# A fused two-block transformer kernel: tile 2 turned under the next unit, weight splits and copies reordered, last rows by column halves

## The chip, the cores and the metric

One core of a Trainium2 chip runs the whole program in one launch. The metric is the device time in microseconds (us); the median of three runs before the change is 1148.49 us (1148.07 to 1149.39).

## What is computed

256 tokens of width 1024, in fp32, go through two blocks. Cut to what matters:

```
h = x + 0.5*rms(swiglu(rms(x)))                       # FFN 1, D_FF 2816
z, xbc, dt, q, k, v, gates = split(rms(h) @ w_in)     # first mixer
y_ssd = rms_by_group(ssd(silu(conv(xbc)), dt) * silu(z)) @ w_branch
y_att = rms(differential_attention(q, k, v)) @ w_branch
h = h + rms((sig(g0)*y_ssd + sig(g1)*y_att) @ w_out)
h = h + 0.5*rms(swiglu(rms(h)))                       # FFN 2
qa, ka, va, q_lat, kv_lat, k_r, ga, gb = split(rms(h) @ w_in_2)
x = h + (sig(ga)*(swa(qa,ka,va) @ w_o1) + sig(gb)*(mla(...) @ w_o2)) @ w_out_2
x = x + swiglu(rms(x))                                # FFN 3
out = rms(x)
```

rms is a root-mean-square norm with a gain row.

## The kernel before

**Units and the ring.** All weights stream in units of 128 x 2048 words (1 MB) through a ring of five slots. SP issues the load of unit c when `w_used` says that unit c - 5 is done. ACT rounds it (`split_hi`, L435 to L443: WH, the high part), DVE subtracts (`split_lo`, L949 to L957: WL, the low part), and PE uses both: `parts` (L1567 to L1569) makes one fp32-like product from three matmuls, high x high, high x low, low x high. Splits are handed out in the order of the units, and where each stands among the other work of ACT and DVE is written out by hand. A split in the wrong place makes PE wait for it, or makes what stands behind it late.

**Tiles.** The tokens are two tiles of 128. H is the residual, XN the normed rows, XTH and XTL the normed rows turned (K on the partitions) and split. Eight PSUM banks: PS[0] to PS[3] are ACC (down projections, two banks for each tile), PS[4] and PS[5] take gate and up products, PS[6] and PS[7] the turned rows.

**FFN.** `ffn` runs 11 steps of 256 hidden columns: units a and b (gate and up, upper and lower half of K) and d (down). The last three d units run by tiles, t = 0 for all three, then t = 1. In step j PE waits for the first tile of step j - 1's hidden rows (`h_ready`), which DVE makes (L999) from ACT's silu (L498).

**Boundary and norm.** Behind each FFN or output product, `boundary(m)` on ACT and DVE makes the post-norm, the residual and the next normed rows, tile 1 then tile 2: ACT squares (L513), rstd (L516, L517), DVE gain and residual (L1015, L1022), ACT squares and rstd of H (`h_rstd`, L464 to L466), DVE XN (L969, L971), PE turns (`turn_normed`, L1501), ACT copies XTH (`xn_hi`, L472), DVE XTL (L978). Meanwhile `norm(n, c)` on PE runs the first two units on tile 1: the high parts of unit c (L1514, L1515), then the low (L1518), then half of unit c + 1 with the first turn of tile 2 in its middle, and then tile 2. n = 1 goes before the first mixer's projection, n = 2 before FFN 2, n = 3 before the second projection, n = 4 before FFN 3. The unit that follows is a narrow one of 32 columns (`narrow`, the step sizes dt) at n = 1, and a chunk of 512 columns at n = 3.

**First mixer.** Projection units XZ (z, dt, x with convolution on DVE, L1166), then q, k, v units beside the scan: for r = 0 to 8, PE, ACT, DVE and POOL each do one step of a group and chunk of the scan, then `beside(r)` units of q, k, v and gate 0. After that 8 heads of attention, each beside one unit of `ssd_w_branch`, and then the gates: for n = 0 to 3, DVE adds the bias (L1327), ACT takes the sigmoid (L740), and both split two units for n = 1 to 3.

**Second mixer.** Rotary terms, latents, 16 heads in two kinds, with g2, kv and output pieces as `cover(q)` between heads.

**End.** Boundary 4 adds FFN 3's rows to H, squares, and DVE scales each tile with gain and rstd (L1484); SP stores each tile (L426).

Of the kernel before, what the change touches and what calls it, by code (L numbers as in the profile page):

```python
# [184 lines left out]
def program(nc, w, out):  # L185
    with ExitStack() as ctx:
# [101 lines left out]
        out_ok = sem("out_ok")  # L288
# [46 lines left out]
        def in2_bank(n, t):  # L335
            return ((4, 5), (0, 1), (4, 5))[n][t]

# [10 lines left out]
        def _(sp):  # L348
# [75 lines left out]
            for t in range(NT):  # L424
                sp.wait_ge(out_ok, t + 1)
                sp.dma_start(x_out[:, t, :], XN[:, t, :]).then_inc(stored, 16)  # L426
            sp.wait_ge(stored, 16 * NT)

        @block.scalar
        def _(act):  # L430
# [89 lines left out]
            def boundary(m, unit, half, next_table=None):  # L520
# [3 lines left out]
                if m in (1, 3):  # L524
# [48 lines left out]
            def x_hi(t):  # L573

                act.wait_ge(ident_loaded, 32)
                for q in range(2):
                    act.wait_ge(xn_turned, 2 * t + q + 1)
                    for k in range(4 * q, 4 * q + 4):
                        ins = nc.scalar.activation(XTH[:, k, t * P:(t + 1) * P], PS[6 + q][:, k % 4 * P:(k % 4 + 1) * P],
                                                   ACT.Copy, scale=COLS[:, k:k + 1])  # L580
                    ins.then_inc(xt_hi, 1)
# [10 lines left out]
            x_hi(0)  # L592
# [16 lines left out]
            for m, (kind, n, h) in enumerate(XZ):  # L609
# [45 lines left out]
            def qkv(u):  # L655
# [8 lines left out]
                elif n < 8:  # L664
                    act.wait_ge(w_used, u + 1)
                    nc.scalar.activation(QK[:, 2 * (n % 4):2 * (n % 4) + 2, n // 4, :],
                                         PS[5 - n % 2][:].rearrange("p (f t) -> p f t", f=2),
# [9 lines left out]
            for r in range(9):  # L677
# [154 lines left out]
            for q in range(18):  # L832
# [5 lines left out]
                if q < 16:  # L838
                    head_exp(q)
                if q in (0, 1, 2, 4, 6, 8, 10, 11, 12, 14, 15, 16, 17):  # L840
# [14 lines left out]
                elif q == 16:  # L855
                    act.wait_ge(tile_half, HALF[U_OSWA])
                    kt_hi(18, U_OSWA)
# [12 lines left out]
            boundary(4, U_END - 1, False)  # L870
# [73 lines left out]
        def _(dve):  # L944
# [89 lines left out]
            def boundary(m, unit, gains=0):  # L1034
# [45 lines left out]
            def x_lo(t):  # L1080

                dve.wait_ge(ident_loaded, 32)
                for q in range(2):
                    dve.wait_ge(xt_hi, 2 * t + q + 1)
                    for k in range(4 * q, 4 * q + 4):
                        a = XTH[:, k, t * P:(t + 1) * P]
                        ins = stt(XTL[:, k, t * P:(t + 1) * P], PS[6 + q][:, k % 4 * P:(k % 4 + 1) * P], COLS[:, k:k + 1],
                                  a.bitcast(F32), ALU.mult, ALU.subtract)
                    ins.then_inc(xt_lo, 1)
# [10 lines left out]
            x_lo(0)  # L1100
            first_unit_lo()
            x_lo(1)
            split_lo()
            split_lo()
# [12 lines left out]
            def step_sizes(c):  # L1117
# [4 lines left out]
                   PS[2][:].rearrange("p (t c) -> p t c", t=NT)[:, :, 0:32], bias, ALU.add).then_inc(dt_raw, 1)  # L1122
# [68 lines left out]
            for r in range(9):  # L1191
# [37 lines left out]
                for _u in range(beside(r)):  # L1229
                    split_lo()  # L1230
            kt_lo(0)
# [919 lines left out]
```

## Time and profile before

| | |
|---|---|
| median of three runs | 1148.49 us |
| the profiled execution | 1148.1 us |
| its span, first to last instruction | 1146.3 us |
| mean granted TensorE clock | 0.992 |
| PE busy | 1116.1 us, 97%, 5748 matmuls |
| PE weight loads | 940.8 us, 82% (beside PE) |
| DVE busy | 697.5 us, 61% |
| ACT busy | 593.6 us, 52% |
| POOL busy | 20.8 us, 2% |
| bytes moved | 202.23 MB, mean 176 GB/s |

Busy time is time in which the engine executes; a share of 97% means that only 3% of the span is open to anything but fewer or faster matmuls. Durations of single matmuls overlap, so their spacing, not their duration, is their cost. L1567 is line 1567 of the kernel before.

### The profile page before, as it was taken

How to read it: one execution, taken by the hardware profiler on the slowest of the kernel's cores; microseconds unless marked ns; L12 is line 12 of the kernel's file. 1: busy time of each engine (PE TensorE's matmuls, PEld its weight loads, DVE VectorE, ACT ScalarE, POOL GpSimd, SP SyncE). 2: the span in 40 equal slices, each digit the busy share in tenths (PEclk: the TensorE clock that was granted, in tenths of full speed). 3: DMA queues.
4: the chain of work that ended last, by engine and by line, in shares of the span. 5: the costliest groups of instructions: out<-in, count | busy, mean ns of one | idle time of the engine just before them, and what ended most of it. 6: DMA issues, size and time to landing. Idle time of an engine off the chain costs nothing.

```text
span 1146.3 us, 14028 instructions
## 1 busy us (share of the span) xinstructions
PE 1116.1 (97%) x5748; PEld 940.8 (82%) x5748; DVE 697.5 (61%) x807; ACT 593.6 (52%) x843; POOL 20.8 (2%) x34
## 2 busy tenths in 40 slices
PE   6999999999999999998999999999999999999997
PEld 4888888899999987777878888887878878888886
DVE  4645555676767777866756455555775667554453
ACT  5543435454567766646445434445766546344442
POOL 0000000000001100000000000000000000000000
PEclk9999999999999999999999999999999999999999
DMA  7755654655566545444466555544634445555550
GB/s 259 251 187 185 189 191 138 225 172 181 182 200 182 171 164 202 133 162 164 149 198 205 185 189 191 190 155 146 205 125 129 153 160 173 192 186 184 184 184 37
DMA packets 132208, 202.23 MB, mean 176 GB/s; under 512 B 5889, under 2 KB 98945, under 8 KB 131889
## 3 DMA queue, kind: packets, MB, share of 16 engines
q1 hardware_dynamic: 129472, 190.68, 51.7%
q0 software_dynamic: 2672, 10.65, 2.8%
q8 instruction: 46, 0.75, 0.3%
q14 instruction: 18, 0.14, 0.0%
HBM read 200.24 MB, written 1.08 MB: 176 GB/s over the span
## 4 chain that ended last, share of the span: by engine, by line
PE 90%; DVE 4%; ACT 4%; issue 1%; DMA 1%; SPq 0%; DVEq 0%; ACTq 0%
PE PS L1567 14%; PE PS L1569 14%; PE PS L1568 14%; PE ACC L1567 13%; PE ACC L1569 13%; PE ACC L1568 13%; ACT WH L442 1%; PE PS L1628 1%; DVE WL L957 1%; PE PS L1501 1%; PE ACC L1815 1%; PE PS L1972 1%; PE PS L1667 1%; PE PS L1971 0%; DMA RAW<-in_w_out 0%
## 5 line engine op out<-in xcount | busy, mean ns | idle before, releaser
L957 DVE TENSOR_TENSOR WL<-RAW,WH 128x2048 fp32r<-128x2048 f32 (+2 forms) x180 | 404.0, 2265 | 112.4 <-ACT WH L442 112.2
L442 ACT ACTIVATE WH<-RAW 128x2048 fp32r<-128x2048 f32 (+2 forms) x180 | 336.0, 1888 | 23.6 <-DMA RAW<-in_w_up 6.2
L1567 PE MATMUL PS<-WH,XTH 128*128 128x512 f32 (+1 forms) x680 | 272.3, 400 | 9.9 <-DVE WL L957 5.4
L1569 PE MATMUL PS<-WH,XTL 128*128 128x512 f32 (+1 forms) x680 | 267.0, 393 | 0.0
L1568 PE MATMUL PS<-WL,XTH 128*128 128x512 f32 (+1 forms) x680 | 266.6, 392 | 0.0
L1567 PE MATMUL ACC<-WH,KTH 128*128 128x512 f32 (+1 forms) x452 | 178.9, 396 | 0.5 <-ACT BUF L778 0.3
L1569 PE MATMUL ACC<-WH,KTL 128*128 128x512 f32 (+1 forms) x452 | 175.7, 389 | 0.0
L1568 PE MATMUL ACC<-WL,KTH 128*128 128x512 f32 (+1 forms) x452 | 175.4, 388 | 0.0
L1567 PEld LDWEIGHTS PS<-WH,XTH 128*128 128x128 f32 x680 | 129.3, 190 | 36.8 <-DVE WL L957 6.1
L1569 PEld LDWEIGHTS PS<-WH,XTL 128*128 128x128 f32 x680 | 129.1, 190 | 27.4
L1568 PEld LDWEIGHTS PS<-WL,XTH 128*128 128x128 f32 x680 | 129.4, 190 | 24.8
L1567 PEld LDWEIGHTS ACC<-WH,KTH 128*128 128x128 f32 x452 | 84.9, 188 | 18.9 <-DVE KTL L1059 1.3
L487 ACT ACTIVATE KTH<-PS 128x512 fp32r<-128x512 f32 x30 | 17.9, 597 | 157.8 <-PE PS L1628 157.8
L1569 PEld LDWEIGHTS ACC<-WH,KTL 128*128 128x128 f32 x452 | 84.8, 188 | 17.7
L1568 PEld LDWEIGHTS ACC<-WL,KTH 128*128 128x128 f32 x452 | 85.0, 188 | 16.1
L990 DVE TENSOR_TENSOR KTL<-PS,KTH 128x512 fp32r<-128x512 f32 x30 | 20.7, 691 | 117.5 <-ACT KTH L487 117.5
L498 ACT ACTIVATE SCR<-PS,RS 128x256 f32<-128x256 f32 x66 | 31.3, 475 | 110.6 <-PE PS L1569 110.5
L999 DVE SCALAR_TENSOR_TENSOR SCR<-PS,RS,SCR 128x256 f32<-128x256 f32 x66 | 31.4, 480 | 41.2 <-ACT SCR L498 41.2
L1567 PE MATMUL ACC<-WH,XTH 128*128 128x512 f32 (+1 forms) x144 | 56.0, 389 | 0.0
L1567 PE MATMUL ACC<-XTH,WH 128*128 128x256 f32 x192 | 55.5, 289 | 0.0
L1568 PE MATMUL ACC<-XTL,WH 128*128 128x256 f32 x192 | 55.0, 286 | 0.0
L1569 PE MATMUL ACC<-XTH,WL 128*128 128x256 f32 x192 | 55.0, 286 | 0.0
(275 smaller groups left out, 1305.1 us busy)
## 6 DMA issues: line engine op xcount, KB each, us to landing
RAW<-in_w_in SPq DMA_DIRECT2D x50, 1024.0 KB, 5.2
RAW<-in_ffn_w_gate SPq DMA_DIRECT2D x44, 512.0 KB, 4.0
RAW<-in_ffn_w_up SPq DMA_DIRECT2D x44, 512.0 KB, 5.0
RAW<-in_ffn_w_down SPq DMA_DIRECT2D x22, 1024.0 KB, 5.0
RAW<-in_w_gate SPq DMA_DIRECT2D x22, 512.0 KB, 4.0
RAW<-in_w_up SPq DMA_DIRECT2D x22, 512.0 KB, 5.0
RAW<-in_w_down SPq DMA_DIRECT2D x11, 1024.0 KB, 4.8
RAW<-in_ssd_w_branch SPq DMA_DIRECT2D x8, 1024.0 KB, 5.0
```

What stands on the lines that cost most here:

```text
L442: nc.scalar.activation(WH[:, s, 0:n], RAW[:, s, 0:n], ACT.Copy).then_inc(w_hi, 1)
L487: nc.scalar.activation(KTH[:, half_of(j)], PS[6][:], ACT.Copy).then_inc(hT_hi, 1)
L498: nc.scalar.activation(SG[:, t, :], PS[4 + t][:, 0:256], ACT.Silu, scale=RS[:, t:t + 1]).then_inc(gate_ok, 1)
L957: tt(WL[:, s, 0:n], RAW[:, s, 0:n], WH[:, s, 0:n].bitcast(F32), ALU.subtract).then_inc(w_lo, 1)
L990: tt(KTL[:, half_of(j)], PS[6][:], KTH[:, half_of(j)].bitcast(F32), ALU.subtract).then_inc(hT_lo, 1)
L999: stt(HS[:, t, :], PS[4 + t][:, 256:512], RS[:, t:t + 1], SG[:, t, :], ALU.mult, ALU.mult).then_inc(h_ready, 1)
L1501: ins = nc.tensor.transpose(PS[6 + q][:, k * P:(k + 1) * P], src[:, t, j * P:(j + 1) * P], IDENT)
L1567: mm(ps, stat_hi, mov_hi, start=first, stop=False)
L1568: mm(ps, stat_hi, mov_lo, start=False, stop=False)
L1569: return mm(ps, stat_lo, mov_hi, start=False, stop=last)
L1628: ins = nc.tensor.transpose(PS[6][:, k * TOK + t * P:k * TOK + (t + 1) * P], HS[:, t, k * P:(k + 1) * P], IDENT)
L1667: ins = nc.tensor.transpose(PS[7][:, k * P:(k + 1) * P], src[:, t, (k0 + k) * P:(k0 + k + 1) * P], IDENT)
```

## The change

Nine edits; no product is added or removed.

1. Start: XTH and XTL of tile 2's two halves have the split of unit 1 between them on ACT and DVE.
2. Boundaries 0 and 2: the split that stood last on ACT and DVE now stands before the squares of tile 2 (ACT) and before XN of tile 2 (DVE). In `norm` at n = 1 and n = 3 PE finishes unit c + 1 on tile 1 first and has tile 1's part of the next unit, in two pieces, around the first turn. dt moves to bank 1, the chunk's first tile stays in bank 0.
3. Boundary 1 on ACT: XTH of tile 2 before the squares of tile 2's H and the table load. In `norm` at n = 2 the first turn stands behind three quarters of the half instead of two.
4. The last z copies stand before a split; the first q unit writes bank 0 and waits for a convolution, not for those copies.
5. Scan's last step: the first K rows (`turn_rows(0)`, `kt_hi(0)`, `kt_lo(0)`) are turned and split between the two halves of gate unit 0, not behind them.
6. Gates: ACT splits two units before the first sigmoid and then 1, 1, 2; DVE one between the two pairs of output scalings, then 1, 1, 1, 2.
7. Second mixer: the keys are turned before the first g2 piece.
8. Heads' end: `kt_hi(18)` and `kt_lo(18)` before that step's split; the first MLA output unit runs tile 2 first, so the wait for the last gate (`g2_kept` 8) comes 12 products later.
9. End: the last unit's tile 2 runs by column halves, so DVE adds, ACT squares and DVE applies the gain for half the columns while PE does the other; rstd comes from both; DVE and ACT scale one half each; two DMAs of 512 columns store it.

```diff
 # ACT, boundary
                     if m == 1:
                         y_rstd(m, unit, 1, half)
-                    h_rstd(m + 1, 0)
-                    h_rstd(m + 1, 1)
-                    nc.scalar.preload_act_table(next_table)
-                    xn_hi(m + 1, 1)
+                        h_rstd(m + 1, 0)
+                        xn_hi(m + 1, 1)
+                        h_rstd(m + 1, 1)
+                        nc.scalar.preload_act_table(next_table)
+                    else:
...
                 y_rstd(m, unit, 1, half)
+                split_hi()
                 h_rstd(m + 1, 1)
                 xn_hi(m + 1, 1)
-                split_hi()
 # ACT, start
-            x_hi(1)
+            x_hi(1, 0)
             split_hi()
+            x_hi(1, 1)
             h_rstd(0, 1)
 # ACT, z units
-                    split_hi()
+                    if (n, h) != (3, 1):
+                        split_hi()
                     if n and h:
                         z_silu(n, c - 3, c)
+                    if (n, h) == (3, 1):
+                        split_hi()
 # ACT, scan and gates
                 for _u in range(beside(r)):
+                    if u == U_GATE0 + 1:
+                        kt_hi(0, 0)
                     qkv(u)
                     u += 1
-            kt_hi(0, 0)
...
-                if n:
-                    split_hi()
+                split_hi()
+                if n in (0, 3):
                     split_hi()
 # ACT, end
-            boundary(4, U_END - 1, False)
+            ln_exp()
+            h_rstd(5, 0)
+            act.wait_ge(last_half, 1)
+            own.wait()
+            own.link(nc.scalar.activation(JUNK[:, 0:512], H[:, 1, 0:512], ACT.Square, accum_out=SS[:, 1:2]))
+            own.inc(nc.scalar.activation(SS[:, 2:3], SS[:, 1:2], ACT.Identity, scale=1.0 / D, bias=EPS))
+            act.wait_ge(last_half, 2)
+            own.inc(nc.scalar.activation(JUNK[:, 512:1024], H[:, 1, 512:1024], ACT.Square, accum_out=SS[:, 3:4]))
+            own.wait()
+            own.link(nc.scalar.activation(RS[:, 1:2], SS[:, 3:4], ACT.Ln, scale=1.0 / D, bias=SS[:, 2:3]))
+            nc.scalar.activation(RS[:, 1:2], RS[:, 1:2], ACT.Exp, scale=-0.5).then_inc(rstd_ok, 1)
+            act.wait_ge(rstd_ok, NT * 6)
+            act.wait_ge(out_gained, 1)
+            nc.scalar.activation(XN[:, 1, 0:512], XN[:, 1, 0:512], ACT.Copy, scale=RS[:, 1:2]).then_inc(out_act, 1)
 # DVE, boundary
+                if m in (0, 2):
+                    split_lo()
                 xn(m + 1, 1)
                 xn_lo(m + 1, 1)
-                split_lo()
+                if m in (1, 3):
+                    split_lo()
 # DVE, output scalings and gates
                        ALU.mult).then_inc(o_ok, 1)
+                if p == 0:
+                    split_lo()
...
-                if n:
+                if n == 3:
                     split_lo()
-                    split_lo()
+                split_lo()
 # DVE, end
+            for h in range(2):
+                dve.wait_ge(w_used, U_END) if h else dve.wait_ge(end_half, 1)
+                a = slice(h * 512, (h + 1) * 512)
+                tt(H[:, 1, a], PS[2 + h][:], H[:, 1, a], ALU.add).then_inc(last_half, 1)
+                dve.wait_ge(last_half, h + 1)
+                tt(XN[:, 1, a], H[:, 1, a], GAIN[:, a], ALU.mult).then_inc(out_gained, 1)
+            dve.wait_ge(rstd_ok, NT * 6)
+            dve.wait_ge(out_gained, 2)
+            ts(XN[:, 1, 512:1024], XN[:, 1, 512:1024], RS[:, 1:2], None, ALU.mult).then_inc(out_ok, 1)
 # PE, norm
-                half(c + 1, 1, 0, 4, (0, 1))
-                turn_normed(n, 1, 0)
-                half(c + 1, 1, 0, 4, (2, 3)).then_inc(chunk_half, 1)
+                if beside:
+                    half(c + 1, 1, 0, 4).then_inc(chunk_half, 1)
+                    pe.wait_ge(w_lo, c + 3)
+                    beside(0)
+                    turn_normed(n, 1, 0)
+                    beside(1)
+                else:
+                    ks = 3 if n == 2 else 2
+                    half(c + 1, 1, 0, 4, range(ks))
+                    turn_normed(n, 1, 0)
+                    half(c + 1, 1, 0, 4, range(ks, 4)).then_inc(chunk_half, 1)
...
-            norm(1, U_XZ)
+            norm(1, U_XZ, lambda h: narrow(U_XZ + 2, 1, SSD_HEADS, 0, range(4 * h, 4 * h + 4)))
...
-            norm(3, U_IN2)
+            norm(3, U_IN2, lambda h: half(U_IN2 + 2, 0, 0, 0, range(2 * h, 2 * h + 2)))
 # PE, heads' end
-                    pe.wait_ge(g2_kept, 8)
                     pe.wait_ge(w_lo, U_OMLA + 1)
-                    rows_part(U_OMLA, [(0, 0)], True, False, half=0)
+                    rows_part(U_OMLA, [(0, 1)], True, False, half=0)
...
-            mla_piece(0, 1)
+            pe.wait_ge(g2_kept, 8)
+            rows_part(U_OMLA, [(0, 0), (1, 0)], True, False, half=0).then_inc(w_used, 1)
```

## Rows read from the trace of the kernel before

**Rows 1.** Waits of PE: engine, line, waited for, us in total, times, longest us.

```profile
PE PS L1567 <- DVE WL L957: 5.4, 3, 3.0
...
PE PS L1501 <- DVE XN L969: 4.4, 2, 2.2
...
PE PS L1567 <- ACT BUF L607: 1.3, 1, 1.3
PE PS L1567 <- DVE XTL L978: 1.1, 1, 1.1
PE PS L1712 <- DVE KTL L1059: 0.5, 1, 0.5
```

**Rows 2.** Busy time by stretches; PEclk is the column behind POOL.

```profile
21.50:25.00 3.50, 3.41 (x8) 2.63 (x9) 1.07 (x2) 2.42 (x2) 0.00 (x0) 0.54 0.78 269
...
223.00:226.60 3.60, 3.60 (x20) 3.60 (x20) 3.21 (x6) 2.28 (x5) 0.00 (x0) 0.53 0.58 165
...
519.00:524.00 5.00, 3.69 (x10) 2.92 (x11) 3.46 (x2) 5.00 (x4) 0.00 (x0) 0.66 0.49 197
...
782.00:787.00 5.00, 4.41 (x17) 3.64 (x18) 1.89 (x3) 0.90 (x2) 0.00 (x0) 0.66 0.00 0
```

**Rows 3.** Timeline of the start: start, us, engine, line, op, [idle before <- releaser].

```profile
16.27 1.14 ACT L579 ACTIVATE XTH<-PS,COLS 128x128 fp32r<-128x128 f32 x4 [1.23 <-PE PS L1501]
...
19.25 2.29 DVE L957 TENSOR_TENSOR WL<-RAW,WH 128x2048 fp32r<-128x2048 f32 x1 [0.68 <-ACT WH L442]
...
21.59 0.63 PE L1567 MATMUL PS<-WH,XTH 128*128 128x512 f32 x1 [2.21 <-DVE WL L957]
```

**Rows 4.** Timeline of norm 1; the last two are the first and last of 48.

```profile
210.01 0.66 PE L1501 MATMUL PS<-TAB,XN 128*128 128x128 f32 x4 [2.21 <-DVE XN L969]
...
217.82 0.18 PE L1567 MATMUL ACC<-WH,XTH 128*128 128x32 f32 x1
...
222.98 0.26 PE L1569 MATMUL ACC<-WH,XTL 128*128 128x32 f32 x1
```

**Rows 5.** Timeline of the gates.

```profile
516.03 3.69 ACT L442 ACTIVATE WH<-RAW 128x2048 fp32r<-128x2048 f32 x2
...
520.31 0.79 PE L1567 MATMUL PS<-WH,XTH 128*128 128x512 f32 x1 [3.02 <-DVE WL L957]
```

**Rows 6.** Timeline of norm 2.

```profile
593.08 1.28 ACT L532 ACT_TABLE_LOAD   x1
...
594.38 1.08 ACT L472 ACTIVATE XTH<-PS 128x512 fp32r<-128x512 f32 x2
...
595.35 1.92 ACT L442 ACTIVATE WH<-RAW 128x2048 fp32r<-128x2048 f32 x1
595.75 0.50 PE L1567 MATMUL PS<-WH,XTH 128*128 128x512 f32 x1 [1.07 <-DVE XTL L978]
...
599.51 0.48 DVE L999 SCALAR_TENSOR_TENSOR SCR<-PS,RS,SCR 128x256 f32<-128x256 f32 x1
```

**Rows 7.** Timeline of boundary 2: H of tile 2.

```profile
778.81 1.28 DVE L1022 SCALAR_TENSOR_TENSOR H<-SCR,RS,H 128x1024 f32<-128x1024 f32 x1
```

**Rows 8.** Timeline of the heads' end: a split and what it waited for.

```profile
918.67 1.91 ACT L442 ACTIVATE WH<-RAW 128x2048 fp32r<-128x2048 f32 x1 [3.62 <-DMA RAW<-in_w_out]
```

**Rows 9.** Timeline of the end; the first two are 12 matmuls.

```profile
1135.98 0.39 PE L1567 MATMUL ACC<-WH,XTH 128*128 128x512 f32 x1
...
1138.48 0.39 PE L1569 MATMUL ACC<-WH,XTL 128*128 128x512 f32 x1
...
1138.97 1.29 DVE L1030 TENSOR_TENSOR H<-ACC,H 128x512 f32<-128x512 f32 x2 [6.87 <-PE ACC L1569]
...
1141.95 1.28 DVE L1484 SCALAR_TENSOR_TENSOR XN<-H,RS,GAIN 128x1024 f32<-128x1024 f32 x1 [0.49 <-ACT RS L466]
...
1143.26 0.36 SPq L426 DMA_DIRECT2D out_x<-XN  x1
```

**Rows 10.** Waits of ACT, the hidden rows of all FFNs.

```profile
ACT KTH L487 <- PE PS L1628: 157.8, 27, 6.3
```

More of the change, by code:

```diff
@@ L336, in in2_bank, with q_bank @@
             return ((4, 5), (0, 1), (4, 5))[n][t]
+        def q_bank(n):
+            return 5 - n % 2 if n else 0
         def v_bank(n, t):
@@ L423, in _ @@
             ffn_loads(U_FFN3, w["w_gate_2"], w["w_up_2"], w["w_down_2"])
[L424 to L427, printed above, removed]
+            sp.wait_ge(out_ok, 1)
+            sp.dma_start(x_out[:, 0, :], XN[:, 0, :]).then_inc(stored, 16)
+            sp.wait_ge(out_ok, 2)
+            sp.dma_start(x_out[:, 1, 512:1024], XN[:, 1, 512:1024]).then_inc(stored, 16)
+            sp.wait_ge(out_act, 1)
+            sp.dma_start(x_out[:, 1, 0:512], XN[:, 1, 0:512]).then_inc(stored, 16)
+            sp.wait_ge(stored, 48)
         @block.scalar
@@ L570, in products, with x_hi @@
                         split_hi()
-            def x_hi(t):
+            def x_hi(t, q):
                 act.wait_ge(ident_loaded, 32)
[L576 to L581, printed above, removed]
+                act.wait_ge(xn_turned, 2 * t + q + 1)
+                for k in range(4 * q, 4 * q + 4):
+                    ins = nc.scalar.activation(XTH[:, k, t * P:(t + 1) * P], PS[6 + q][:, k % 4 * P:(k % 4 + 1) * P],
+                                               ACT.Copy, scale=COLS[:, k:k + 1])
+                ins.then_inc(xt_hi, 1)
             def first_unit_hi():
@@ L1078, in products, with x_lo @@
                             split_lo()
-            def x_lo(t):
+            def x_lo(t, q):
                 dve.wait_ge(ident_loaded, 32)
[L1083 to L1089, printed above, removed]
+                dve.wait_ge(xt_hi, 2 * t + q + 1)
+                for k in range(4 * q, 4 * q + 4):
+                    a = XTH[:, k, t * P:(t + 1) * P]
+                    ins = stt(XTL[:, k, t * P:(t + 1) * P], PS[6 + q][:, k % 4 * P:(k % 4 + 1) * P], COLS[:, k:k + 1],
+                              a.bitcast(F32), ALU.mult, ALU.subtract)
+                ins.then_inc(xt_lo, 1)
             def first_unit_lo():
@@ L1580, in channels, with narrow @@
                 ins.then_inc(w_used, 1)
-            def narrow(c, bank, wide):
+            def narrow(c, bank, wide, t, ks):
                 s = slot(c)
-                pe.wait_ge(w_lo, c + 1)
-                for t in range(NT):
-                    for k in range(KD):
-                        ws = slice(k * wide, (k + 1) * wide)
-                        ins = parts(PS[bank][:, t * 256:t * 256 + wide], x_hi(k, t), x_lo(k, t),
-                                    WH[:, s, ws], WL[:, s, ws], k == 0, k == KD - 1)
-                ins.then_inc(w_used, 1)
+                for k in ks:
+                    ws = slice(k * wide, (k + 1) * wide)
+                    ins = parts(PS[bank][:, t * 256:t * 256 + wide], x_hi(k, t), x_lo(k, t),
+                                WH[:, s, ws], WL[:, s, ws], k == 0, k == KD - 1)
+                return ins
             def rows_part(c, order, first, last, banks=0, half=0):
@@ L1653, in ffn @@
                         half_at = 2 if n == 2 else (s + n) % 2
-                        rows_part(c, [(0, t)], False, n == 2, half=half_at)
-                        if t and n == 2 and then:
-                            then()
-                        ins = rows_part(c, [(1, t)], False, n == 2, half=half_at)
+                        if t and n == 2 and f == 2:
+                            for h in range(2):
+                                for k in range(2):
+                                    ws = slice(k * D + h * 512, k * D + (h + 1) * 512)
+                                    ins = parts(PS[2 + h][:], LASTH[:, 2 * k + 1], LASTL[:, 2 * k + 1], WH[:, slot(c), ws],
+                                                WL[:, slot(c), ws], False, k == 1)
+                                if h == 0:
+                                    ins.then_inc(end_half, 1)
+                        else:
+                            rows_part(c, [(0, t)], False, n == 2, half=half_at)
+                            if t and n == 2 and then:
+                                then()
+                            ins = rows_part(c, [(1, t)], False, n == 2, half=half_at)
                         if t:
@@ L1755, in _ @@
                 elif kind == "dt":
-                    narrow(c, 2, SSD_HEADS)
+                    narrow(c, 1, SSD_HEADS, 1, range(KD)).then_inc(w_used, 1)
                 elif n and h:
```

68 lines of the change are left out of this document (42 added, 26 removed).

## The prediction

> **What bounds the kernel now.** Read first the busy table of the page: PE is busy 1116.1 of 1146.3 us, no other engine above 61%. A change that adds and removes no matmul can therefore win only where PE is dry, where its clock is low, or behind its last matmul. Then the waits of PE [rows 1]: the five rows hold 12.7 us. What else PE waits for is the first DMA and the first splits, before its first product, where the change does nothing, and five waits of 0.2 to 0.4. Most of the 12.7 lies in four places: at 21.59, 210.01, 520.31 and 782.59 us PE is dry for 2.21, 2.21, 3.02 and 2.21 us. Then the clock by stretches [rows 2]: 1.00 everywhere except four pieces, and there PE ran at 1.2 instead of 2.4 GHz for about 3.4 us. In the first, 8 matmuls started in 3.5 us where 15 fit at the full-clock spacing of (1138.48 - 1135.98) / 11 = 0.227 us [rows 2, 9]: one such stretch costs 7 x 0.227 = 1.6 us. Three of the four begin in or just behind a dry place; the fourth, at 223 us, comes right behind 48 matmuls of 32 columns, and the dry place at 210 us was followed by none for 13 us. So dry time and clock are removed together, but not for certain. Last, the tail: 1138.5 to 1146.3 us.
>
> **The change part by part.** All times are of the profiled execution: 1148.1 us, its span 1146.3 and 1.8 around it; the median shown is 1148.49, 0.4 above.
>
> *Start.* ACT is free at 16.27 - 1.23 = 15.04 us and now splits unit 1 (1.9 us) before the last quarter of XTH; DVE follows at 16.97 instead of 19.25 and ends at 19.3 [rows 3]. PE ran out at 21.59 - 2.21 = 19.38: the gap goes, and with it the half-clock stretch behind it. What is late next: XTH's last quarter, the squares (1.6), the table load and unit 2's split stand one behind the other on ACT, so WL of unit 2 is ready at 25.0 and the first hidden tile at 25.5, while PE is there at 19.4 + 24 x 0.227 = 24.85. Before, it was there at 21.59 + 5.46 + 1.6 = 28.7. Gain 28.7 - 25.5 = 3.2.
>
> *Turn of tile 2 before the first projection (norm 1).* The dry 2.21 us up to 210.01 are filled with 6 half-unit products and 12 of the 32-column ones (spacing (222.98 - 217.82) / 47 = 0.110) [rows 4]; 12 more stand between the two turns. The split of the narrow unit that DVE now does before XN is 128x256, 0.4 us, under its wait for RS. Counted on PE from 206.3: 12 x 0.227 + 1.3 + 0.4 + 1.3 + 0.4 + 24 x 0.227 + 2.6 = 14.2, so the projection begins at 220.6 and not at 223.1: 2.4. The low clock at 223 may stay (now 24 narrow products before it and 24 around the turns). If it goes, 1.6 more, less about 0.4, since the step-size chain on DVE is then late for the first turn of x. I take the middle: 3.0, ends 2.4 and 3.6.
>
> *Z copies and the first q unit.* The 1.35 us wait for both silu copies [rows 1] goes, since the unit writes bank 0. The split moved behind the copies delays DVE's cumulative columns by 2 us, and the scan's first mask has some 1.5 us of room: 1.2, ends 0 and 1.35.
>
> *End of scan.* K turns one unit earlier, so the KTL wait of 0.45 goes [rows 1], but the 4 turns no longer cover the second gate copy, and DVE is the later engine there. 0, ends -0.4 and 0.45.
>
> *Gates.* Unit 79 was split behind the first sigmoid at 516.03, its WL came at 520.3, PE was dry from 517.29 [rows 5]. Now ACT splits 79 and 80 right after the table load (510.75 to 514.4) and DVE the first between the two pairs of scalings, by 515.0; 80 by 519.6, 81 by 523.1, each before PE asks (523.0, 528.7). All of the 3.02 goes and the low clock of that place (0.66 over 5 us, so 1.4 of the 1.6): 4.4, lower end 2.5.
>
> *Boundary 1 (norm 2).* PE's waits of 0.41 and 1.07 shrink: XTH is copied when the turn is done, at 592.9 and not at 594.38, so PE goes on at 594.3 instead of 595.75 [rows 6]: +1.45. But the second squares (1.6 us) and the table load now stand between XTH and the split of unit 92. XTH ends at 594.65; squares and rstd to 596.2; table to 597.45; split to 599.4, where it began at 595.35. DVE's split and the first hidden tile behind it, which ended at 599.51 + 0.48 = 599.99, shift by the same 2.1 to 602.1. PE, which needs that tile, is there at 594.3 + 24 x 0.227 = 599.75 and is dry for 2.35 us; before, it was there at 601.2 and did not wait. Net -0.95. A dry place of this size was followed by the low clock at 21.5, 519 and 782, not at once at 210: I take half of 1.6, so -1.7; ends +1.4 (should the hidden tile be ready in time) and -2.6.
>
> At this place a rule speaks. The row shows that the table load holds ACT for 1.28 us and the next copy starts 1.30 after it [rows 6]. The Trainium skill (ScalarE: Activation LUTs, What ACT_TABLE_LOAD costs) says that a switch costs about 1283 ns plus a drain of about 1380. With the drain the new wait of PE would be an estimated 1.4 us longer and the sum 1.4 smaller. The trace has the duration, so the sum goes by it.
>
> *Boundary 2 (norm 3).* ACT splits unit 125 at 777.9 to 779.8, free there. DVE, done with H at 778.81 + 1.28 = 780.1 [rows 7], splits it for 2.29 us and only then makes XN, 0.55 later than before. PE, dry from 782.59 - 2.21 = 780.4, has 6 more products of its half now, is through at 781.6, waits 0.75 for WL at 782.35, then covers the turns with 12 products that it does later today. Of the 2.21 us 1.45 are won, of the low clock behind them 1.6 (a wait of 0.75 should not bring it: those of 1.07 and 1.35 did not), and 0.3 of slow first matmuls and fewer edges: 3.4, ends 1.4 and 3.6. DVE's queue behind that split is XN and XTL of tile 2, for which PE waits; the cover is 12 x 0.227 = 2.7 us, their chain 2.9 to the last, so little is left over.
>
> *Keys turned before the gate piece.* The 0.3 wait for the last copy goes: 0.3. *Attention's end.* The g2 wait (0.33) goes since tile 1's banks are free; but the next K copy is held on ACT by a split that starts only when a weight load has landed, at 918.67 [rows 8], and ends in PE's product at 921.85 either way: 0, upper end 0.33.
>
> *Last rows by halves.* Now: last matmul 1138.48, add of both halves, squares and rstd, XN, DMA at 1143.26, end 1146.3 [rows 9]. After: the second half's add 1138.97 to 1139.66, its square (half as long) to 1140.4, rstd to 1140.9, XN by two engines in halves to 1141.5, DMAs at 1141.4 and 1141.8. The bytes are the same, so the end comes 3.0 behind the first issue: 1144.4. Gain 1.9, ends 1.2 and 2.3.
>
> *Queues.* SP's loads wait for the same units in the same order, each as early as PE is; only the output's one DMA becomes two. POOL issues nothing else and is passed by nothing.
>
> **Sum.** 3.2 + 3.0 + 1.2 + 0 + 4.4 - 1.7 + 3.4 + 0.3 + 0 + 1.9 = 15.7. 1148.1 - 15.7 = 1132.4, and with the 0.4 to the median 1132.8 us.
>
> **The rivals.**
> A. *The new wait does not appear and the clock stays up*: +2.35 + 0.8 at norm 2 and +0.6 at norm 1: 1129.0. For it: every wait of PE but these is short. Against: the count at boundary 1 leaves 2.35 us of lateness, no rounding.
> B. *Stalls moved, not removed*: the split stream of ACT and DVE is late elsewhere by what PE wins, in the scan (slack of 1.5 us only), at unit 83 (ready within 0.1 of its use) and at norm 1, and three low-clock stretches stay. Price 1.2 + 0.6 + 3 x 1.6 = 6.6 off: 1139.4. For it: ACT and DVE chains end within a few tenths of PE in scan and heads. Against: DVE 61%, ACT 52% busy.
> C. *Slower*: FFN 2 starts with ACT and DVE 2.35 us late and they never catch up, so each of its steps stalls PE by that: 10 x 2.35 = 23.5 more: 1156. It decides when ACT's wait for the turned hidden rows falls to zero; today that wait is up to 6.3 us in a step, 157.8 in 27 [rows 10], which speaks against it.
> D. *The reordering does nothing*: the dry places are made by something the profile hides behind the named releaser. 1147. Against: the releasers' own rows end within 0.1 us of PE's starts [rows 3, 5].
>
> **How the numbers follow.** Forecast 0.64 (own range 1130 to 1136), A 0.10, B 0.20, C 0.03, D 0.03. The range 1129 to 1138.5 holds the forecast, A's edge and most of B. A difference under 0.2% (2.3 us) can't be told from none here. Faster: forecast, A, B, part of D: 0.94; same 0.03; slower 0.03.
>
> **What would show it.** In the changed kernel's waits: no PE wait for WL at the second unit or in the gates; none over 1 us for XN; one new wait of about 2.3 us for the first hidden tile of FFN 2, near 587 us plus what is won, and one near 0.7 at 25 us and at the third boundary. The clock table has one or two pieces near 0.5 in place of four, behind the narrow products or that new wait. The last DMA is issued 3.4 us behind the last matmul, now 4.8. Wrong if a boundary shows DVE's split ending after PE has run dry by more than 1 us at norm 3, if FFN 2 starts without a wait, or if the scan's mask is the releaser of a PE wait.

## The result, and the profile after

The changed kernel takes 1132.8 us (median of four runs, 1131.38 to 1134.39) against 1148.29 for the kernel before beside it (1148.07 to 1149.39): ratio 0.9859, 95% interval 0.984 to 0.9877. A second series gave 1132.72 against 1148.33, ratio 0.9867 (0.9848 to 0.9886). The forecast was 1132.8 us, and faster.

The profiled execution of after took 1134.39 us, the slowest of its four; its span is 1132.6 us (1146.3 before), mean granted clock 0.996 (0.992), PE busy 1112.1 us, 98%, the same 5748 matmuls. The waits of PE, to be laid beside [rows 1] (engine, line, waited for, us in total, times, longest):

```profile
PE PS L1620 <- DVE WL L1129: 4.1, 1, 4.1
PE PS L1620 <- DVE SCR L1029: 2.7, 2, 2.2
PE PS L1913 <- ACT BUF L677: 0.7, 1, 0.7
PE ACC L1620 <- DVE WL L987: 0.6, 1, 0.6
PE ACC L1620 <- DVE KTL L1092: 0.5, 1, 0.5
```

The first is the wait for the first split of all, before the first product (3.3 in before); the change does nothing there. Of the rows of before, DVE XN L969 (4.4) and ACT BUF L607 (1.3) are gone, DVE WL L957 (5.4) is down to 0.19 at 507.35 us and the 0.6 at norm 3, and DVE XTL L978 (1.1) to 0.3. New is the second row, 2.7 us: 2.2 of it is one wait at FFN 2. The places, on PE's timeline (start, us, line, operation, idle before and its releaser):

```profile
26.27 0.47 PE L1620 MATMUL PS<-WH,XTH 128*128 128x512 f32 x1 [0.51 <-DVE SCR L1029]
...
432.08 0.50 PE L1913 MATMUL PS<-QK 64*128 64x128 f32 x4 [0.69 <-ACT BUF L677]
...
507.35 0.47 PE L1620 MATMUL PS<-WH,XTH 128*128 128x512 f32 x1 [0.19 <-DVE WL L987]
...
593.16 0.47 PE L1620 MATMUL PS<-WH,XTH 128*128 128x512 f32 x1 [2.22 <-DVE SCR L1029]
...
774.33 0.50 PE L1620 MATMUL ACC<-WH,XTH 128*128 128x512 f32 x1 [0.62 <-DVE WL L987]
...
910.11 0.50 PE L1620 MATMUL ACC<-WH,KTH 128*128 128x512 f32 x1 [0.45 <-DVE KTL L1092]
```

The clock by stretches, beside [rows 2] (us; PE, PEld, DVE, ACT, POOL busy; PEclk; DMA share; GB/s):

```profile
19.00:26.00 7.00, 6.76 (x30) 5.03 (x28) 4.57 (x7) 4.88 (x8) 0.00 (x0) 1.00 0.70 228
208.00:213.00 5.00, 5.00 (x27) 4.43 (x27) 1.66 (x3) 2.91 (x4) 0.00 (x0) 0.68 0.41 157
219.00:224.00 5.00, 5.00 (x31) 5.00 (x31) 3.33 (x6) 4.03 (x6) 0.00 (x0) 0.66 1.07 357
592.00:597.00 5.00, 3.84 (x19) 3.21 (x20) 5.00 (x5) 3.42 (x3) 0.00 (x0) 1.00 0.85 277
774.00:779.00 5.00, 4.67 (x24) 3.90 (x25) 2.38 (x5) 1.32 (x3) 0.00 (x0) 1.00 0.00 0
```

Two pieces of half clock (stretches at 1.2 GHz) are left of four, both in norm 1 and not behind a dry place: they begin at 209.84 and 220.08 us, 0.3 and 0.4 us behind the last of 12 and of 24 matmuls of 32 columns on end. The gates, FFN 2, norm 3 and, from 15.3 us on, the start run at full clock, also behind the 2.22 us. What a piece costs is read from stage lengths (the stages are those of the table below). With one, two and three pieces norm 1 takes 34.90, 36.49 and 38.05 us in traces with PE's old order there; with none and one, norm 3 takes 31.96 and 33.49: 1.5 to 1.6 us a piece. In norm 1's new order one piece costs 1.2 (32.39 against 31.21) and two cost 2.8. The granted clock, 3.4 us at half speed each, would give 1.70.

One slow stretch the table of clocks doesn't show. In every trace of this study the first products start 0.43 us apart where the later ones start 0.23 apart, while the clock column says 1.00. Two of the kernel before:

```profile
14.03 0.63 PE L1568 MATMUL PS<-WL,XTH 128*128 128x512 f32 x1
14.46 0.63 PE L1569 MATMUL PS<-WH,XTL 128*128 128x512 f32 x1
```

The spacing falls at 15.0 us there, 5.0 behind the first product, and at 15.3 in after, 4.5 behind it.

A comparison by stages uses landmarks on PE that both kernels have (first product, first turn of norm 1, first turn of x, first scores, first turn of norm 2, first turn of hidden rows in FFN 2, first turn of norm 3, rotary turn, first scores of the second mixer, last matmul). Stages without a piece repeat from trace to trace within 0.1 us, so this is finer than the medians. Two are coarser: the start (188.9 to 189.1 in the old order), and the heads' stage, which takes 314.2 to 314.6 us with the change as it is and 314.4 to 314.7 with none of its edits in that stage.

| stage | before | after | won | forecast |
|---|---|---|---|---|
| first product to norm 1 | 191.26 | 188.11 | 3.15 | 3.2 |
| norm 1 to first turn of x | 34.90 (1 piece) | 33.98 (2 pieces) | 0.92 | 3.0 |
| to first scores (z, q, scan) | 199.92 | 199.17 | 0.75 | 1.2 |
| to norm 2 (end of scan, gates) | 149.94 | 144.86 | 5.08 | 4.4 |
| norm 2 to first hidden turn | 18.01 | 19.07 | -1.06 | -1.7 |
| FFN 2 | 169.80 | 169.82 | 0.0 | 0 |
| norm 3 and on | 33.49 | 30.39 | 3.10 | 3.4 |
| keys | 16.47 | 16.05 | 0.42 | 0.3 |
| heads, output, FFN 3 | 314.67 | 314.23 | 0.44 | 0 |
| last matmul to the end | 7.82 | 6.10 | 1.72 | 1.9 |

The sum is 14.5; the span fell by 13.7, since the first product of this execution started 0.8 us later (10.82 against 10.02).

### The profile page after: what moved, and what is told of

It reads as the page before. It is cut to its first block, busy times and chain, and to the rows that moved or that the text cites. A ratio compares the mean times of both kernels' runs of the same rounds, so it can differ in the third digit from the quotient of the medians.

```text
span 1132.6 us, 14039 instructions
## 1 busy us (share of the span) xinstructions
PE 1112.1 (98%) x5748; PEld 938.5 (83%) x5748; DVE 697.5 (62%) x809; ACT 594.6 (53%) x847; POOL 20.8 (2%) x34
## 4 chain that ended last, share of the span: by engine, by line
PE 94%; ACT 2%; DVE 2%; DMA 1%; issue 1%; SPq 0%; DVEq 0%; ACTq 0%
PE PS L1620 14%; PE PS L1622 14%; PE PS L1621 14%; PE ACC L1620 14%; PE ACC L1622 14%; PE ACC L1621 14%; PE PS L1679 1%; PE ACC L1882 1%; DVE WL L987 1%; PE PS L1546 1%; PE PS L2039 1%; DMA RAW<-in_ffn_w_up 1%; ACT WH L449 1%; PE PS L1727 1%; PE PS L2038 0%
## 5 line engine op out<-in xcount | busy, mean ns | idle before, releaser
L1620 PE MATMUL ACC<-XTH,WH 128*128 128x256 f32 x208 | 60.0, 288 | 0.0
L1621 PE MATMUL ACC<-XTL,WH 128*128 128x256 f32 x208 | 59.6, 286 | 0.0
L1622 PE MATMUL ACC<-XTH,WL 128*128 128x256 f32 x208 | 59.5, 286 | 0.0
```

The costliest lines, as they stand in the source:

```text
L1620: mm(ps, stat_hi, mov_hi, start=first, stop=False)
L1621: mm(ps, stat_hi, mov_lo, start=False, stop=False)
L1622: return mm(ps, stat_lo, mov_hi, start=False, stop=last)
```

## The experiments

**Boundary 1, from the changed kernel.** The split of FFN 2's next unit, moved early (the old place stays at m = 3 alone):

```diff
                     if m == 1:
                         y_rstd(m, unit, 0, half)
+                        split_hi()
                     xn_hi(m + 1, 0)
...
-                    split_hi()
+                        split_hi()
                     return
```

> The changed kernel with one move on ACT at boundary 1: the split of the unit of FFN 2's second step stands behind the first post-norm rstd (ACT idle there for 4.30 us up to 577.58) instead of behind the last squares and the table load. Theory (the new 2.22 us wait of PE for the first hidden tile is made by that split standing at 588.38 to 590.3 on ACT, with DVE's half of it behind): ACT's silu comes at 588.4, the hidden tile at 589.4, PE asks at 590.95 and does not wait; 1132.8 - 2.2 = 1130.6 us, interval about 0.2% wide. Rival (DVE's chain or the product's own arrival makes the tile late, the split only stands beside it): the wait stays at 1.5 to 2.2 us, 1132 to 1133. Rival 2 (the wait only moves to the next step, whose splits are as late): 1132.8 and a new wait of some 2 us near 597.

Measured: 1129.49 us (1128.72 to 1130.48), ratio to before 0.9827 (0.9809 to 0.9845). The rows of after (first fence) and of this kernel (second), ACT and DVE:

```profile
587.09 1.28 ACT L540 ACT_TABLE_LOAD   x1
588.38 1.92 ACT L449 ACTIVATE WH<-RAW 128x2048 fp32r<-128x2048 f32 x1
590.20 0.45 ACT L505 ACTIVATE SCR<-PS,RS 128x256 f32<-128x256 f32 x1
...
592.54 0.87 DVE L1029 SCALAR_TENSOR_TENSOR SCR<-PS,RS,SCR 128x256 f32<-128x256 f32 x2
```

```profile
583.58 1.28 ACT L541 ACT_TABLE_LOAD   x1
584.88 0.47 ACT L505 ACTIVATE SCR<-PS,RS 128x256 f32<-128x256 f32 x1
...
585.38 0.48 DVE L1030 SCALAR_TENSOR_TENSOR SCR<-PS,RS,SCR 128x256 f32<-128x256 f32 x1 [0.40 <-ACT SCR L505]
```

The silu stands right behind the table load now, and DVE starts on the hidden tile 1.8 us behind that load's start, where it was 5.5 behind. PE has no wait there; the stage from norm 2 to the first hidden turn is 16.53 us, 2.54 less than in after and 1.48 less than before the change. So the cause of the wait is shown, it did not move to the next step, and the price of the edit at norm 2 was only the place of one split. The medians are 3.3 apart; the rest fits the clock, 0.997 to 1.0 in the four runs of this kernel and 0.996 to 0.999 in those of after.

The edit of boundary 1 on ACT taken back, with the three quarters of the half before the first turn kept:

```diff
-                        h_rstd(m + 1, 0)
-                        xn_hi(m + 1, 1)
-                        h_rstd(m + 1, 1)
-                        nc.scalar.preload_act_table(next_table)
-                    else:
-                        h_rstd(m + 1, 0)
...
+                    h_rstd(m + 1, 0)
+                    h_rstd(m + 1, 1)
+                    nc.scalar.preload_act_table(next_table)
+                    xn_hi(m + 1, 1)
```

> The changed kernel with boundary 1 on ACT in the order of before (both squares and the table load ahead of XTH of tile 2), the first turn still behind three quarters of the half. Theory (that edit alone brings both the 1.45 us gained before the turn and the 2.22 us wait behind it, net -1 to -1.7): 1131.8 us, ends 1131.1 and 1132.1; waits for XTL of 1.0 to 1.4 back, none for the first hidden tile. Rival (the wait comes from the three quarters or from elsewhere, the ACT order is a gain): 1134.3, wait for the hidden tile stays.

Measured: 1131.33 us (1130.39 to 1133.3), ratio 0.9844 (0.9826 to 0.9863); the stage is 18.05 us, against 18.01 before and 19.07 in after. The wait for XTL is back, 1.77 us where 1.0 to 1.4 were expected, and there is none for the hidden tile:

```profile
586.56 0.50 PE L1615 MATMUL PS<-WH,XTH 128*128 128x512 f32 x1 [1.77 <-DVE XTL L1003]
```

So this edit, as it stood, cost 1.0 us, and with the split moved it gives 1.5: the sign hung on what stood behind it on ACT. The three quarters are worth nothing by themselves (18.05 and 18.01): the time saved before the turn comes back in the wait behind it.

**The 32-column matmuls spread out**, for the two pieces in norm 1:

```diff
-                if beside:
+                if n == 1:
+                    half(c + 1, 1, 0, 4, range(2))
+                    pe.wait_ge(w_lo, c + 3)
+                    beside(0, range(0, 3))
+                    half(c + 1, 1, 0, 4, (2,))
+                    beside(0, range(3, 5))
+                    turn_normed(n, 1, 0)
+                    beside(0, (5,))
+                    half(c + 1, 1, 0, 4, (3,)).then_inc(chunk_half, 1)
+                    beside(0, (6, 7))
+                elif beside:
                     half(c + 1, 1, 0, 4).then_inc(chunk_half, 1)
...
+                    for h in range(2):
+                        pe.wait_ge(xt_lo, 4 * n + 3 + h)
+                        for k in range(4):
+                            ins = half(c + h, h, 1, 5, (k,))
+                            if k == 3:
+                                ins.then_inc(w_used, 1)
+                            ins = beside(1, (4 * h + k,))
```

> The changed kernel with the 48 matmuls of 32 columns before the first projection spread between the wide ones of tile 1's and tile 2's half units, in runs of 3 to 9 instead of 12, 12 and 24. Same products. Theory (the two half-clock pieces of the changed kernel, 208 to 213 and 218 to 223 us, follow from the dense runs of narrow matmuls): both go, 2 x 1.6 us where a run has both; the repeats of the changed kernel spread over 1131.4 to 1134.4, so the median falls by 1.6 to 3.2, to 1131.2 to 1129.6, and the spread shrinks. Rival (the clock falls there by the turns and dry tenths around them, or by chance): both pieces stay, 1132.8 within 0.7.

Measured: 1134.33 us (1133.41 to 1134.48), ratio 0.9867 (0.9849 to 0.9884). The times of both expectations fail. The clock over the stretch is 1.00, but so it is in four traces of kernels that keep the dense runs (below), so this says nothing on the cause; and the order costs time. Against the kernel with the early split, whose norm 1 has full clock too (31.19 us), its stage takes 32.68. ACT and PE of this kernel, then ACT of the other:

```profile
219.03 1.91 ACT L449 ACTIVATE WH<-RAW 128x2048 fp32r<-128x2048 f32 x1 [4.74 <-DMA RAW<-in_w_in]
...
230.26 0.63 ACT L643 ACTIVATE SCR<-SCR 128x512 f32<-128x512 f32 x1 [3.36 <-DVE SCR L1200]
...
230.94 0.66 PE L1823 MATMUL PS<-TAB,SCR 128*128 128x128 f32 x4 [1.15 <-ACT SCR L643]
```

```profile
217.46 1.91 ACT L449 ACTIVATE WH<-RAW 128x2048 fp32r<-128x2048 f32 x1 [3.62 <-DMA RAW<-in_w_in]
```

The spread matmuls stand between unit c's last products, so that unit is done and the load into its slot lands 1.6 us later, and ACT's split, which waits for that load, holds the step sizes, the convolution and the turn of x behind it: 219.03 against 217.46, 230.94 against 229.38. Its trace also has a piece behind the 2.21 us wait at FFN 2, where that of after has none.

**One part of the change alone, in the kernel before.** Gates:

```diff
-                if n:
-                    split_hi()
+                split_hi()
+                if n in (0, 3):
                     split_hi()
# DVE
+                if p == 0:
+                    split_lo()
...
-                if n:
+                if n == 3:
                     split_lo()
-                    split_lo()
+                split_lo()
```

> The kernel before with the gates' edit alone (ACT splits two units ahead of the first sigmoid, DVE one between the pairs of scalings). Theory: the dry 3.02 us at 517 to 520 and the half clock behind it go together: 4.4 us faster than before, lower end 3.0 (dry time alone), upper 4.9 (what the two traces show over this stretch). Rival (the half clock stays, it comes from the thin work of the preceding stretch): 3.0. Rival 2 (ACT and DVE owe the time in the following boundary): under 2.

Measured: 1142.04 us (1141.3 to 1145.22) against 1149.03, ratio 0.994 (0.9921 to 0.9958), so 4.8 to 9.1 us faster. The stage from scores to norm 2 is 145.08 us instead of 149.94: 4.86 is what the edit gives. The rest of the profiled difference lies elsewhere: this trace has the same dry 2.21 us before norm 3 as [rows 2] and no half clock behind it.

```profile
778.19 0.66 PE L1503 MATMUL PS<-TAB,XN 128*128 128x128 f32 x4 [2.21 <-DVE XN L969]
```

```profile
778.00:783.00 5.00, 4.81 (x25) 4.07 (x26) 2.19 (x4) 2.89 (x3) 0.00 (x0) 1.00 0.00 0
```

The start (`x_hi(1, 0)`, `split_hi()`, `x_hi(1, 1)`, and the same on DVE), norm 1 and norm 3 (each with its split moved and PE's order as in the change), and the end, each alone:

> The kernel before with the start's edit alone (the last quarter of XTH and XTL behind the split of unit 1). Theory: the dry 2.21 us at 21.6 and the half clock behind it go, the first hidden tile is late by 0.5 instead: 3.2 us faster than before, ends 2.8 and 3.6. Rival (the half clock is chance and stays somewhere): 1.6 to 1.9. Rival 2 (ACT pays it back in the first steps of FFN 1): under 1.

> The kernel before with norm 1's edit alone (narrow unit's tile 1 around the first turn of tile 2, its split ahead of XN). Theory (dry 2.21 us filled with work that is done anyway): from the first turn before norm 1 to the first turn of x the time falls from 34.9 us to 31.2 where no half clock falls in it, to 34.0 where two pieces do (as in the two traces of the changed order seen so far), so 0.9 to 3.7 faster, most likely 2.5. Rival (two pieces always come with the new order): 0.9. Rival 2 (the step sizes' chain on DVE becomes late for the first turn of x): a wait of 1 us there.

> The kernel before with norm 3's edit alone (first tile of the next chunk around the first turn of tile 2, its split ahead of XN on DVE). Theory: 1.6 of the dry 2.21 us go, one wait of 0.6 for WL stays, and the half clock behind it goes if it was there: 3.1 faster than a run that has the piece at 782 us, 1.5 than one that has not (the kernel with the gates' edit alone had the same dry 2.21 us and no half clock behind them): between 1.5 and 3.1. Rival (the dry time is only moved to the turns: XN is 0.5 late behind the split): 0.5 or less.

> The kernel before with the end's edit alone (last rows by column halves). Theory: from the start of the last matmul to the end of the span 6.1 us instead of 7.8, so 1.7 faster, ends 1.4 and 2.0. Rival (the end is set by the output's last DMA, whose bytes are the same and which are now two): 0.5 or less, with the issue earlier and the end not.

Measured against 1148.82 us (29 runs, 1147.54 to 1153.18):

| alone | median, us | ratio (95%) | its stage | same stage, before |
|---|---|---|---|---|
| start | 1146.18 | 0.9973 (0.9961 to 0.9984) | 187.83 | 191.26 with a piece, 188.9 to 189.1 without |
| norm 1 | 1143.97 | 0.9952 (0.9935 to 0.9968) | 32.39, 1 piece | 34.90 with 1 piece, 36.49 with 2 |
| norm 3 | 1146.21 | 0.9977 (0.9964 to 0.9989) | 30.43 | 33.49 with a piece, 31.9 without |
| end | 1147.49 | 0.9978 (0.9966 to 0.9991) | 6.09 | 7.82 |

All four are faster; the medians alone could not rank them, since runs of the kernel before differ by more than five microseconds, with mean clocks of 0.992 or 0.993 up to 1149.1 us and of 0.989 from 1151.4 us on. The stages can. Norm 1 gives 2.5 us at an equal number of pieces (34.90 - 32.39, and 36.49 - 33.98); its median shows more than any theory allowed, and its trace has no half clock at the start, where nothing was edited: PE was dry there for 1.65 us, not 2.21, as in the traces of norm 3 and the end alone. In these three the matmuls came to full speed 3.3 to 3.8 us behind the first product and not 5.0, so the turns of tile 2, and ACT's copies and split behind them, were early: PE could go on 11.02 us behind the first product (norm 1 alone) and not 11.57. Of the 2.15 us between 191.26 and 189.11, 0.55 is this and 1.6 the piece. Norm 3 is 3.06 where a piece goes with it and 1.5 where not; one wait for WL of 0.61 stays, and XN is not late:

```profile
783.06 0.50 PE L1581 MATMUL ACC<-WH,XTH 128*128 128x512 f32 x1 [0.61 <-DVE WL L960]
```

The end comes earlier with the issue, though the last tile's bytes are the same: last matmul, then first and second DMA of that tile. The span ends 2.7 us behind the second; before the change it ended 3.0 behind the single one.

```profile
1138.26 0.39 PE L1594 MATMUL ACC<-WH,XTL 128*128 128x512 f32 x1
...
1141.25 0.36 SPq L428 DMA_DIRECT2D out_x<-XN  x1
1141.65 0.43 SPq L430 DMA_DIRECT2D out_x<-XN  x1
```

Edits 4, 5, 7 and 8 were not run alone; what is said of them below is read from waits and stages.

**The changed kernel once more.**

> The changed kernel unchanged, once more, on the chip of the next three. Theory (what differs from run to run in it is only how many half-clock pieces of 1.7 us fall into a run, since the same dry place had one in some traces and none in others): 1131 to 1135 us, in steps of about 1.7, mean granted clock 0.996 to 0.999, the slower runs those of the lower clock. Rival (runs differ by their dry places): same clock in all runs, other waits.

Measured: 1131.0, 1131.67, 1133.76 and 1134.99 us, with mean clocks 0.999, 0.999, 0.996, 0.996. Its profiled execution (span 1129.2, 3.4 less than the first one's) has every wait of the fences above within 0.1 us, but for the start's and no piece at all:

```profile
208.00:213.00 5.00, 5.00 (x30) 4.36 (x30) 2.50 (x3) 3.85 (x4) 0.00 (x0) 1.00 0.22 84
219.00:224.00 5.00, 5.00 (x44) 5.00 (x44) 4.49 (x10) 3.70 (x9) 0.00 (x0) 1.00 0.78 257
589.00:594.00 5.00, 4.45 (x22) 3.70 (x23) 5.00 (x5) 3.46 (x4) 0.00 (x0) 1.00 0.73 231
```

Norm 1 takes 31.21 us here and 33.98 there: the same instructions, waits and order, and 2.8 us apart by two pieces.

**Dry places made by repeats.** The first hidden tile computed several times over, in a step where the stream is steady:

```diff
+                        for _ in range(DOSE.get((f, j), 0) if t == 0 else 0):
+                            own.link(stt(HS[:, t, :], PS[4 + t][:, 256:512], RS[:, t:t + 1], SG[:, t, :], ALU.mult, ALU.mult))
```

> The kernel with the early split at boundary 1, and in steps 3 and 7 of each FFN the first hidden tile computed 14, 16; 15, 17; 16, 18 times more on DVE (the same values again), each about 0.5 us, against a slack of 6.1 us before PE asks for the tile: dry places of about 0.9, 1.9; 1.4, 2.4; 1.9, 2.9 us in a steady stream of wide matmuls. Theory (the half clock follows long dry places and not short ones: in the traces so far it came behind 5 of 5 of 3.02 us, 9 of 14 of about 2.2, 0 of 4 of 1.6 to 1.8 and none shorter): a piece of 1.7 us behind the place of 2.9, perhaps behind that of 2.4, none behind 0.9 and 1.4. Rival (the pieces belong to the boundaries, where turns and narrow or split-starved work stand together, and not to dry time): none behind any of the six. Rival 2 (every dry place can bring it, by chance): pieces behind short ones too.

> As the kernel before it, with the repeats in other places: 17, 15; 18, 14; 15, 17, so dry places of about 2.4, 1.4; 2.9, 0.9; 1.4, 2.4 us. Theory: a half-clock piece behind 2.9, perhaps behind the two of 2.4, none behind 0.9 and 1.4. Rival: none at all, or the pieces stand at the same steps as in the other kernel whatever their dry time.

Measured: 1148.22 and 1146.86 us, one run of each kernel. Each repeat is 0.52 us, and each dry place came out 0.2 to 0.3 us longer than planned. Of the first kernel PE's rows at four places and the clock behind them, of the second two:

```profile
147.02 0.47 PE L1625 MATMUL PS<-WH,XTH 128*128 128x512 f32 x1 [2.17 <-DVE SCR L1034]
645.12 0.47 PE L1625 MATMUL PS<-WH,XTH 128*128 128x512 f32 x1 [1.65 <-DVE SCR L1034]
715.27 0.47 PE L1625 MATMUL PS<-WH,XTH 128*128 128x512 f32 x1 [2.69 <-DVE SCR L1034]
1082.55 0.50 PE L1625 MATMUL PS<-WH,XTH 128*128 128x512 f32 x1 [3.24 <-DVE SCR L1034]
```

```profile
147.00:152.00 5.00, 4.98 (x17) 4.00 (x18) 2.47 (x2) 0.00 (x0) 0.00 (x0) 0.66 0.54 187
645.00:650.00 5.00, 4.88 (x23) 4.07 (x24) 3.25 (x3) 1.41 (x2) 0.00 (x0) 1.00 0.63 207
715.00:720.00 5.00, 4.73 (x23) 3.97 (x24) 3.37 (x4) 1.28 (x2) 0.00 (x0) 1.00 0.47 162
1082.00:1087.00 5.00, 4.45 (x13) 3.48 (x14) 3.00 (x3) 0.00 (x0) 0.00 (x0) 0.66 0.41 145
```

```profile
649.27 0.47 PE L1625 MATMUL PS<-WH,XTH 128*128 128x512 f32 x1 [3.21 <-DVE SCR L1034]
```

```profile
649.00:654.00 5.00, 4.73 (x23) 3.98 (x24) 3.36 (x4) 1.28 (x2) 0.00 (x0) 1.00 0.36 125
```

Half clock came behind 2.17, 2.20 and 3.24 us and not behind 1.13 (twice), 1.65, 1.68 (twice), 2.69, 2.72 (twice) and 3.21. So the first rival (boundaries only) is wrong, the third (short ones too) has nothing for it, and the theory holds in its lower half only: a longer dry place does not make it certain. Apart from the clock, a dry place costs about 0.3 us above the idle time shown: FFN 2, where neither kernel has a piece, takes 174.69 and 174.70 us against 169.83 in the kernel without repeats, 4.9 more for 4.34 of idle time in two places.

**A version that beats both.** The early split, and at the heads' end the K copy ahead of a split that waits for a load:

```diff
+                if q == 17:
+                    kt_hi(19, U_OSWA + 2)
                 if q in (0, 1, 2, 4, 6, 8, 10, 11, 12, 14, 15, 16, 17):
                     split_hi()
...
-                elif q == 17:
-                    kt_hi(19, U_OSWA + 2)
```

> The kernel with the early split at boundary 1, and besides the copy of the K rows of the heads' end (kt_hi 19) ahead of that step's split on ACT, which waits for a weight load. Theory: the copy comes at 901 instead of 903.0, PE's wait of 0.65 us for KTL goes and nothing is late behind it: 0.65 faster than the version without it, 1128.8, and about 3.9 faster than the changed kernel of the same call. Rival (the split is late by the copy and its own product waits instead): no gain, 1129.5.

Measured: 1128.33 us (1127.65 to 1129.21), ratio to before 0.9823 (0.9808 to 0.9837); the changed kernel in the same series 0.9867. The copy comes 2.0 us earlier and PE does not wait:

```profile
900.96 0.60 ACT L564 ACTIVATE KTH<-PS 128x512 fp32r<-128x512 f32 x1 [2.99 <-PE PS L1773]
901.45 1.91 ACT L449 ACTIVATE WH<-RAW 128x2048 fp32r<-128x2048 f32 x1
```

```profile
901.18 1.92 ACT L449 ACTIVATE WH<-RAW 128x2048 fp32r<-128x2048 f32 x1 [3.60 <-DMA RAW<-in_w_out]
903.00 0.57 ACT L564 ACTIVATE KTH<-PS 128x512 fp32r<-128x512 f32 x1
...
904.35 0.50 PE L1621 MATMUL ACC<-WH,KTH 128*128 128x512 f32 x1 [0.65 <-DVE KTL L1093]
```

From the first WL wait of norm 3 to the K turn behind the first output unit it is 0.98 us shorter than without that edit (139.56 against 140.54). The medians of the two, 1128.33 and 1129.49, are from two series and agree with it, but do not show it alone.

## Why the prediction was right

*Start.* As reckoned: the dry 2.21 us and the piece behind it go, the first hidden tile is late by 0.51 (forecast 0.65). 3.15 against 3.2. But the forecast took the piece as certain, and of the five traces with the old start three have none; against those the edit is worth 0.8 to 1.3. That the trace of before had one is luck. Its reading "1.00 everywhere except four pieces" also passes over the 5 us of half-speed products at the start; its price of 1.6 us for a piece is what the stages give.

*Norm 1.* The dry place is gone and nothing waits. At equal clock the edit gives 2.5, the forecast's lower end being 2.4 with the piece at 223 us kept. What failed is the middle of 3.0: it took half the chance that the piece goes, and did not see that two could come. The profiled execution had two and won 0.9; the second one had none and won 3.7.

*Z copies, end of scan.* PE's lead over before grows from 3.27 us at the first turn of x to 4.50 at the products behind the last scan step (424.25 and 419.75): 1.2 as forecast. Then the first scores wait 0.69 instead of 0.25 for the second gate copy, and 0.45 of KTL goes: 0, with both terms as named.

*Gates.* 4.86 against 4.4. All of the 3.02 goes. The clock was put at 1.4, where a piece costs 1.6 by the stages above, and about 0.3 was left out: what the repeats show a dry place to cost beyond its idle time.

*Norm 2.* The step most at risk. Forecast: PE dry 2.35 us for the first hidden tile, net -0.95 without clock. Measured: 2.22 and -1.06. The reckoning of ACT's queue behind the moved copy was right instruction by instruction: XTH, squares, table load, split, silu. The 0.8 for half a piece of clock was too much for the first execution (none) and fair as a mean: of three traces with this wait one has a piece. The drain that the Trainium skill (ScalarE: Activation LUTs, What ACT_TABLE_LOAD costs) puts behind a load of tables is not in the trace: the split starts 1.29 us behind the start of the load at 587.09; with it the wait would have been an estimated 3.6 us.

*Norm 3.* 3.10 against 3.4; the wait for WL 0.62 instead of 0.75.

*Keys, heads' end.* 0.42 against 0.3. The 0.44 of the last stage but one lies within what that stage varies by where nothing was changed, so the forecast's 0 stands. At the heads' end the wait for g2 went (0.33); the wait for KTL, which was under 0.15 in before (the product at 921.85), is 0.45, since the K copy is still held by the split: what is won at the one comes back at the other, as named.

*Last rows.* 1.72 against 1.9. The last DMA is issued 1129.89 - 1126.50 = 3.39 us behind the last matmul, as forecast, and ends the span 2.7 later:

```profile
1126.50 0.39 PE L1622 MATMUL ACC<-WH,XTL 128*128 128x512 f32 x1
...
1126.93 0.69 DVE L1524 TENSOR_TENSOR H<-ACC,H 128x512 f32<-128x512 f32 x1
1128.97 0.49 DVE L1529 TENSOR_SCALAR XN<-XN,RS 128x512 f32<-128x512 f32 x1 [0.62 <-ACT RS L897]
...
1129.48 0.36 SPq L431 DMA_DIRECT2D out_x<-XN  x1
1129.89 0.43 SPq L433 DMA_DIRECT2D out_x<-XN  x1
```

*The sum.* 15.7 forecast, 15.5 between the medians. By stages the profiled execution has 14.5 in place of 15.7: 2.1 is missing in norm 1 and 0.5 in z and scan, 0.6 too much was taken off at norm 2, end of scan and gates gave 0.7 more, and the rest is tenths. That the median hit to a tenth is partly luck: the eight runs of the changed kernel lie between 1131.0 and 1135.0 us, in part by their pieces.

*The rivals.* A had one half right (norm 1 at full clock, in the second trace) and one wrong (the wait is there). B did not come: in scan and heads the only waits that grew by over 0.2 us are the first scores' (0.25 to 0.69) and KTL's at the heads' end, and pieces were two, not three. C: FFN 2 takes 169.82 us with the late start and 169.80 without; the lateness is taken up within the first step. D: the dry places went with their named releasers.

## What to carry to other kernels

An instruction that is moved forward on a queue moves all that it passes back by its length: reckon the queue to the next thing that the bound engine asks for, and look for an idle stretch of the same queue for what was passed (here 4.3 us of ACT's idle time took the split, and turned -1.06 into +1.48). Half clock is a term of its own, with a size (1.2 to 1.6 us a piece here) and a chance, not a price that goes with every dry place; compare two versions by stages between landmarks and by equal numbers of pieces, and the medians only after that. Filler that covers a turn must not stand before the last product of a ring slot's unit, or a load and all behind it is late.

## What the runs showed of the hardware that was not expected

Over all fourteen traces, once PE had come to full speed: a dry place of up to 1.77 us was never followed by half clock (seven of 1.6 to 1.8); those of 2.16 to 2.22 us were in 11 of 17 cases, of 2.69 to 2.72 in 0 of 3, of 3.02 to 3.24 in 6 of 7. The same place with the same wait to 0.03 us has it in one trace and not in another (210, 590 and 780 us). A piece lasts 3.4 us (twice 6.8, two on end, in norm 1).

Half clock also comes while PE is busy. Of the stretch of 32-column matmuls nine traces have one or two pieces and five have none. With 48 on end (the five traces with the old order) there was always one, and it began between 1.4 us before the last of the 48 and 0.3 us behind it, 13 to 15 us after a dry place of 2.2. With 12, 12 and 24 on end (eight traces) there were two in three traces, one in one and none in four, each 0.2 to 0.7 us behind the last of a run. With 9 at most on end (one trace) there was none. What decides is open.

At the start, where PE had been dry for 3.3 to 4.1 us just before, the first products ran at half speed in all fourteen traces, until 13.2 to 16.4 us. How long this lasted mattered in the old order (0.55 us in FFN 1's stage, above) and hardly in the new one: with full speed 3.2 and 5.5 us behind the first product that stage takes 187.84 and 188.06 us.
